# Expert weights fetched in 4 MB pieces from the fifth expert on, with four early-loaded pieces moved to other experts

## The reference

```python
def expert_block(args):
    tok, wr, e = args
    hb = xpad[tok] @ mlp1_w[e] + mlp1_b[e]              # 1024 -> 2048
    yb = clamped_swiglu(hb) @ mlp2_w[e] + mlp2_b[e]     # 1024 -> 1024
    return yb * wr[:, None].astype(yb.dtype)
```

## Time and profile before

| what | value |
|---|---|
| median of 3 runs | 1349.01 us (1348.27 to 1352.93) |
| the profiled execution's own time | 1347.37 us |
| its span, first to last instruction | 1345.6 us, so 1.8 us lie around it |
| mean granted TensorE clock | 0.981 of full speed |
| TensorE matmul busy | 1249.0 us (93%) |
| DVE, ACT, POOL busy | 357.0, 191.1, 60.3 us |
| read from HBM | 440.74 MB |

### The profile page before, as it was taken

How to read it: one execution, slowest core, us unless ns; L and a number is a source line. 1 busy time by engine, 2 the same in 40 slices (tenths; PEclk the granted TensorE clock), 3 DMA queues, 4 the chain that set the end, 5 groups by cost and what they waited for, 6 DMA issues and landing times.

```text
span 1345.6 us, 18997 instructions
## 1 busy us (share of the span) xinstructions
PE 1249.0 (93%) x7700; PEld 636.5 (47%) x7700; DVE 357.0 (27%) x843; ACT 191.1 (14%) x434; POOL 60.3 (4%) x107
## 2 busy tenths in 40 slices
PE   6999789879888999998989999999998999989897
PEld 5888677758776343332333334333233332323332
DVE  3555642332224522121212112212121111212111
ACT  2232234411221000000000000000000000000000
POOL 8200001101000000000000000000000000000000
PEclk9999889989998999999999999999999999999999
DMA  6333110009534999999999999999999999999996
GB/s 241 129 126 125 64 64 33 33 33 379 235 140 169 396 427 428 429 429 429 429 429 427 427 427 427 427 429 428 429 428 429 429 429 429 429 429 429 429 428 285
DMA packets 34916, 442.56 MB, mean 329 GB/s; under 512 B 3888, under 2 KB 4016, under 8 KB 5296
## 3 DMA queue, kind: packets, MB, share of 16 engines
q1 hardware_dynamic: 34704, 441.28, 78.4%
q0 software_dynamic: 160, 0.52, 0.1%
HBM read 440.74 MB, written 1.05 MB: 328 GB/s over the span
## 4 chain that ended last, share of the span: by engine, by line
PE 58%; DMA 34%; DVE 4%; issue 1%; ACT 1%; POOL 0%; SPq 0%; DVEq 0%; ACTq 0%
DMA sb_ring<-in_mlp_w 34%; PE ps L917 20%; PE ps L334 8%; PE ps L976 7%; PE ps L885 2%; PE ps L751 2%; PE ps L661 2%; PE ps L786 2%; PE ps L894 2%; PE ps L532 2%; PE ps L933 1%; PE ps L824 1%; PE ps L953 1%; PE ps L350 1%; PE ps L407 1%
## 5 line engine op out<-in xcount | busy, mean ns | idle before, releaser
L917 PE MATMUL ps<-sb_ring,sb_hT 128*64 128x512 f32 x1984 | 445.6, 597 | 35.4 <-DMA sb_ring<-in_mlp_w 34.4
L917 PEld LDWEIGHTS ps<-sb_ring,sb_hT 128*64 128x64 f32 x1984 | 134.7, 137 | 322.1 <-issue 252.8
L976 PE MATMUL ps<-sb_ring,sb_hT 128*64 128x512 f32 x1024 | 228.4, 596 | 0.0
L1491 DVE TENSOR_SCALAR sb_early<-ps 128x256 f32<-128x256 f32 x64 | 27.2, 425 | 645.1 <-PE ps L917 645.0
L976 PEld LDWEIGHTS ps<-sb_ring,sb_hT 128*64 128x64 f32 x1024 | 71.6, 137 | 133.3 <-issue 131.5
L1532 ACT ACTIVATE sb_early<-sb_early 128x256 f32<-128x256 f32 (+2 forms) x69 | 28.2, 408 | 524.1 <-DVE sb_early L1491 516.7
L334 PE MATMUL ps<-sb_hnT,sb_wsl 128*128 128x256 f32 x288 | 64.8, 386 | 3.7 <-DVE sb_hnT L1061 3.7
L1532 ACT ACTIVATE sb_early<-ps 128x512 f32<-128x512 f32 (+4 forms) x46 | 23.6, 515 | 287.9 <-PE ps L976 267.8
L885 PE MATMUL ps<-sb_early,sb_hnT 128*128 128x128 f32 x512 | 61.9, 281 | 0.8 <-DVE sb_early L1370 0.8
L334 PEld LDWEIGHTS ps<-sb_hnT,sb_wsl 128*128 128x128 f32 x288 | 55.8, 194 | 12.4 <-DVE sb_hnT L1061 4.1
L894 PE MATMUL ps<-sb_early 64*128 64x512 f32 x248 | 61.6, 615 | 0.0
(11 more groups left out here) (353 smaller groups left out, 1043.8 us busy)
## 6 DMA issues: line engine op xcount, KB each, us to landing
sb_ring<-in_mlp_w SPq DMA_DIRECT2D x186, 2048.0 KB, 22.0
sb_wsl<-in_w_front SPq DMA_DIRECT2D x31, 1024.0 KB, 4.8
sb_ring<-in_mlp_w SPq DMA_DIRECT2D x4, 1024.0 KB, 14.9
sb_wsl<-in_mlp_w SPq DMA_DIRECT2D x3, 1024.0 KB, 4.8
sb_wsl<-in_w_values SPq DMA_DIRECT2D x1, 1120.0 KB, 5.1
sb_hT<-in_x_T SPq DMA_DIRECT2D x2, 512.0 KB, 5.9
sb_wsl<-in_w_front SPq DMA_DIRECT2D x2, 512.0 KB, 6.8
sb_ox<-in_mem_T SPq DMA_DIRECT2D x1, 1024.0 KB, 11.5
```

What stands on the lines that cost most here:

```text
L917: mm = pe.matmul(psum[64 * half:64 * half + 64, 4 + n, :], xgT[:, k, SLOTS * par:SLOTS * par + SLOTS], w[:, at + 512 * half:at + 512 * hal ...
L976: mm = pe.matmul(psum[64 * o2:64 * o2 + 64, 7, :], actT[:, 2 * n + m, 64 * q:64 * q + 64], ring[:, at + 512 * o2:at + 512 * o2 + 512], sta ...
L1491: dve.tensor_scalar(gl, psum[:, 4 + n, 0:256], 7.0, None, ALU.min).then_inc(sem("glu"), 1)
```

## The change

From item 4 (`SINGLE`) on, SP joins pieces 0 and 1, 2 and 3, and 4 and 5 into one DMA of 4 MB each (128 rows of 32 KB). It issues such a DMA when both of its pieces are free, and TensorE waits for it only at the even piece. Items 0 to 3 keep 2 MB pieces. The pieces loaded ahead are now those of experts 8, 12, 16 and 20; in these items piece 1 comes alone. In the last item pieces 0 and 1 come as one DMA, the others as before. TensorE's program now has items 0 to 3 and 8 to 21 written out. In the last item `scatter` and the first transposes stand between pieces 2 and 3, and the second half's transposes between the two halves of the second layer.

```diff
-        AHEAD_AT = 10
+        AHEAD_AT = (8, 12, 16, 20)
+        SINGLE = 4
+        MIDDLE = AHEAD_AT[-1] + 2
...
+                ahead = sum(i >= at for at in AHEAD_AT) if stage == "middle" else 0
+                if c % 2 == 0:
+                    loads = i + 1 if c or stage == 0 else i + 2 - ahead
+                    pe.wait_ge(sem(f"piece_in_{c}"), loads * 16)
+                elif stage in (0, 1):
+                    pe.wait_ge(sem(f"piece_in_{c}"), (i + 1) * 16)
+                elif stage == "middle" and i in AHEAD_AT and c == 1:
+                    pe.wait_ge(sem("piece_in_1"), (SINGLE + ahead) * 16)
+                elif stage == "last" and c > 1:
+                    pe.wait_ge(sem(f"piece_in_{c}"), (SINGLE + 1) * 16)
...
                     if 1024 * (k + 1) % PIECE == 0:
                         mm.then_inc(sem("piece_used"), 1)
+                        if stage == "last" and n and k == 3:
+                            scatter(1 - par)
+                            turn_act(i, 0)
...
+                if stage == "last":
+                    pe.wait_ge(sem("selgT"), i + 1)
+                    second(i, 0, stage)
+                    turn_act(i, 1)
+                    second(i, 1, stage)
+                    return
...
-            item(0, 0, 0)
-            item(0, 1, 1)
+            for i in range(SINGLE):
+                item(i // 2, i % 2, min(i, 1))
...
-            with pe.Fori(1, AHEAD_AT // 2) as j:
+            with pe.Fori(SINGLE // 2, AHEAD_AT[0] // 2) as j:
                 for par in range(2):
-                    item(j, par, 1)
-            for a in range(4):
-                item((AHEAD_AT + a) // 2, a % 2, 1, ahead=a)
-                for bank in range(4) if a == 3 else ():
+                    item(j, par, "pairs")
+            for i in range(AHEAD_AT[0], MIDDLE):
+                item(i // 2, i % 2, "middle", ahead=AHEAD_AT.index(i) if i in AHEAD_AT else None)
+                for bank in range(4) if i == AHEAD_AT[-1] else ():
...
-            def item(i, e, which=range(PIECES)):
+            def pairs(i, e, which=(0, 2, 4)):
+
+                for c in which:
+                    sp.wait_ge(sem("piece_used"), i * PIECES + (c + 2 - PIECES))
+                    piece(e, c, at=(PIECE * c, PIECE * (c + 2)))
+
+            def singles(i, e, which=range(PIECES)):
+
                 for c in which:
                     sp.wait_ge(sem("piece_used"), i * PIECES + (c + 1 - PIECES))
                     piece(e, c)
...
+            for i in range(2, SINGLE):
+                singles(i, i)
+            with sp.Fori(SINGLE, AHEAD_AT[0]) as i:
+                pairs(i, i)
+            for i in range(AHEAD_AT[0], MIDDLE):
+                if i in AHEAD_AT:
+                    singles(i, i, (1,))
+                pairs(i, i, (2, 4) if i in AHEAD_AT else (0, 2, 4))
...
-            for c in range(PIECES - 1):
+            sp.wait_ge(sem("piece_used"), before_last * PIECES + 2)
+            piece(e, 0, at=(0, 2 * PIECE))
+            for c in range(2, PIECES - 1):
                 sp.wait_ge(sem("piece_used"), before_last * PIECES + (c + 1))
                 piece(e, c)
```

More of the change, by code:

```diff
@@ L921, in hidden, with turn_act, second, item @@
                         mm.then_inc(sem("piece_used"), 1)
+                        if stage == "last" and n and k == 3:
+                            scatter(1 - par)
+                            turn_act(i, 0)
                     elif stage == 0 and n == 0 and k == 1:
                         mm.then_inc(sem("half_used"), 1)
-            def item(j, par, stage, ahead=None, last=False):
+            def turn_act(i, n):
+                pe.wait_ge(sem("swiglu"), i * 2 + 2 + n)
+                pe.wait_ge(sem("act_out"), i * 2 + 1 + n)
+                for m in (2 * n, 2 * n + 1):
+                    mm = pe.transpose(psum[:, 6, m * P:(m + 1) * P], actv[:, m * P:(m + 1) * P], ident[:, :])
+                mm.then_inc(sem("act_turned"), 1)
+            def second(i, n, stage):
+                pe.wait_ge(sem("act_out"), i * 2 + 2 + n)
+                for q in range(2):
+                    for m in range(2):
+                        at = 16384 + 4096 * n + 2048 * q + 1024 * m
+                        if at % PIECE == 0:
+                            landed(i, at // PIECE, stage)
+                        if stage == "last" and n and q and m == 0:
+                            pe.wait_ge(sem("late_in"), 16)
+                        for o2 in range(2):
+                            mm = pe.matmul(psum[64 * o2:64 * o2 + 64, 7, :],
+                                           actT[:, 2 * n + m, 64 * q:64 * q + 64],
+                                           ring[:, at + 512 * o2:at + 512 * o2 + 512],
+                                           start=at == 16384, stop=at == 24576 - 1024)
+                        if (at + 1024) % PIECE == 0:
+                            mm.then_inc(sem("piece_used"), 1)
+            def item(j, par, stage, ahead=None):
                 i = j * 2 + par
@@ L948, in item @@
                     pe.wait_ge(sem("gate_taken"), 1)
[L949 to L962, removed]
+                if stage == "last":
[4 more added lines that the diff above has]
+                    return
+                turn_act(i, 0)
+                if first:
+                    for g in range(4):
+                        r = slice(NE * g, NE * g + NE)
+                        pe.matmul(psum[:, g, :], gateT[r, g // 2, :], bias2[r, :], start=True, stop=False,
+                                  skip_group_check=True)
+                else:
+                    scatter(1 - par)
+                turn_act(i, 1)
+                if par:
                     pe.wait_ge(sem("selected"), j + 2)
@@ L1993, in piece_ahead @@
                 lo = 2048 * half
-                sp.dma_start(aheads[n][half], a["mlp_w"][AHEAD_AT + n, :, lo:lo + 2048]) \
+                sp.dma_start(aheads[n][half], a["mlp_w"][AHEAD_AT[n], :, lo:lo + 2048]) \
                   .then_inc(sem(f"ahead_in_{n}"), 16)
@@ L2017, in _ @@
             piece(1, 0, at=(PIECE // 2, PIECE))
-            item(1, 1, range(1, PIECES))
-            with sp.Fori(2, AHEAD_AT) as i:
-                item(i, i)
-            for i in range(AHEAD_AT, AHEAD_AT + 4):
-                item(i, i, range(1, PIECES))
-            sp.sem_inc(sem("piece_in_0"), 16 * 4)
-            piece(AHEAD_AT + 4, 0)
-            item(AHEAD_AT + 4, AHEAD_AT + 4, range(1, PIECES))
-            with sp.Fori(AHEAD_AT + 5, NE - 2) as i:
-                item(i, i)
+            singles(1, 1, range(1, PIECES))
+            for i in range(2, SINGLE):
[6 more added lines that the diff above has]
+                pairs(i, i, (2, 4) if i in AHEAD_AT else (0, 2, 4))
+            sp.wait_ge(sem("piece_used"), MIDDLE * PIECES + (2 - PIECES))
+            sp.sem_inc(sem("piece_in_0"), 16 * len(AHEAD_AT))
+            with sp.Fori(MIDDLE, NE - 2) as i:
+                pairs(i, i)
             sp.wait_ge(sem("tabled"), 1)
@@ L2031, in _ @@
                 e = sp.value_load(tabi[0:1, bass.ds(i + 1, 1)], min_val=0, max_val=NE - 1)
-                item(i, e)
+                pairs(i, e)
             e = sp.value_load(tabi[0:1, bass.ds(last_item + 1, 1)], min_val=0, max_val=NE - 1)
             before_last = sp.value_load(tabi[0:1, 61:62], min_val=NE - 2, max_val=ITEMS - 1)
-            for c in range(PIECES - 1):
+            sp.wait_ge(sem("piece_used"), before_last * PIECES + 2)
+            piece(e, 0, at=(0, 2 * PIECE))
+            for c in range(2, PIECES - 1):
                 sp.wait_ge(sem("piece_used"), before_last * PIECES + (c + 1))
```

10 lines of the change are left out of this document (4 added, 6 removed).

## The result

The changed kernel takes 1352.11 us in the median, before 1348.69 us (20 runs each, measured side by side); the ratio is 1.0022, 95% interval 1.0012 to 1.0032, so 1.6 to 4.3 us slower. That is inside the 0.5% that I called no change, and inside the range. The sum in the prediction had +0.3 us. The profiled execution has a span of 1349.1 us, 3.5 us over that of before.

What follows compares the result with a forecast made beforehand. The weights' DMA queue, always holding work, was taken to bound the kernel. Terms -2.6 + 1.3 + 1.6 = +0.3 us on the profiled 1347.37 gave 1347.7, as a median 1349.3 us; range 1344.0 to 1354.0.

Steps and rivals of the forecast that it cites:

- 4 MB pieces: Joined DMAs from item 4 on: 78 joins save 33 ns each, -2.6 us, bounds -0.6 to -4.4.
- D: Rival on the joined DMAs: rows are cut into 16 KB packets, only completions are saved; +2.9, 1351.9 us; chance 0.18.
- C: Rival, faster: long DMAs flow at a better rate than the packet count says; 1346.6 or 1342 us; chance 0.13.
- its smaller case: In C: the step from 16 to 32 KB gives 0.7% on 78 DMAs, -5.3 us, 1346.6 in all.
- Items written out: TensorE's program: 12 more instruction packets in the DMA queues at 0.11 us each, +1.3 us, bounds 0.5 and 2.6.
- Moved early pieces: Pieces loaded ahead at items 8, 12, 16, 20: same bytes, queue never dry, so worth nothing by itself.
- The queue with 4 MB pieces: Steady items: tightest issue, pieces 4+5 of items 8, 12, 16, 20, has 1.9 us to spare; 0 us.
- rival B: Slower: the queue runs dry in the four early-loaded items; 1351.3, or 1355.7 us and more; chance 0.09.
- its two cases: In rival B: each place lacks 0.5 us, +2.0; or 3.5 us of delay at each place, +6.4.
- the mark of a wrong prediction: Rate in the windows 432 GB/s or more, or below 425 around items 8, 12, 16 or 20.
- The last item: Joined first pieces and new order: second layer ends 14.9 us after piece 3 is seen, before 13.3; +1.6 us.
- the second layer needs piece 4: Last item: piece 4 is there, 3.51 us more; second transposes and ACT's copy 1.0; last 3.51 end 14.9 after piece 3.

Runs made afterwards that it cites:

- waits half filled: U with the second half's bias matmuls started again twice in odd items' waits, except behind an early-loaded item; ratio to the kernel before 0.9991.
- U: Changed kernel with the whole last item as before (old order, pieces 0 and 1 as two DMAs); ratio to the kernel before 0.9998.
- odd items: U with the early-loaded pieces at items 9, 13, 17 and 21 in place of 8, 12, 16 and 20; ratio to the kernel before 0.9979.
- four kernels with the same middle: Changed kernel (1.0022), it with the last item's old order (1.0003), it with last pieces 0 and 1 as two DMAs (1.0022), and U (0.9998).

## Why the prediction was right, and where it was not

The call (no change within 0.5%) and the range held. The sum had +0.3 us, and +3.4 us were measured. That it came so near is partly luck: the gain of the change was put 3.3 us too small, and three losses were put too small as well (by 0.7 to 1.5, 1.7 and about 4 us), and these errors mostly cancel.

- **4 MB pieces.** Predicted -2.6 us, 33 ns for each of 78 DMAs. The loop's rates, 77.69 against 77.09 MB, make 9.71 of 9.79 us: 76 ns for each, -5.9 us, and splitting the DMAs cost 4.9 us. The packet count over 7 and 16 us was too coarse a ruler (its own bounds, -0.6 to -4.4, don't hold the measured value), and it carried the step from 8 to 16 KB over to 32 KB. Of the rivals, D (16 KB packets) is refuted by the packet count, though its time, 1351.9, is nearest to the measured one; of C its smaller case, 0.7% on these DMAs, happened. An item's period in the loop is 29.13 us, where I had said 29.27.
- **Items written out.** Predicted +1.3, measured 2.0 to 2.8 us at 1.0020 and 1.0021. The mechanism fits (the delay stands where the written-out items are and nowhere else), the size was short; the bound was 2.6. The Trainium skill, "Runtime: NRT & Kernel Launch", section "Instruction fetch mechanics", calls a block's price mostly hidden. TensorE shows no stall in 700 to 880 before, in agreement with it; for the time of this kernel, whose DMA queue is full, the 0.17 us or more of each packet is not hidden.
- **Moved early pieces.** Predicted 0 by themselves; with 2 MB pieces the two ratios agree (1.0020 and 1.0021), within some 2 us.
- **The queue with 4 MB pieces.** Predicted never dry, 1.9 us to spare. This step failed: rival B's place was right, and its price, about 4 us over the four places, lies between its two cases (2.0 and 6.4 us). The rate of 386 GB/s lies below the 425 that I had named as the mark of a wrong prediction, and the 432 of the loop (1110 to 1290) meets the mark on the other side. What took the spare time in part is TensorE's clock, which fell after two waits of 1.5 and 2.3 us; I had worked out such waits and not asked what they do to the clock. It is not all: groups without a fall still take 0.5 us more than the written-out items explain, with the waits half filled (clock 1.00 in the mean of that stretch) U still lacked 1.8 MB, and with odd items little was lost although the clock fell at the start of each group. By the groups of the profiles it is the larger part (1.9 us with a fall, 0.5 without); the kernel with the half filling, 0.9 us better than U with an uncertainty of 2, doesn't settle it. The margin was taken from one isolated 1 MB DMA and from mean landings. That the 16 queues end at different times, the first of them dry while the mean is not, is my guess, and not tested.
- **The last item.** Predicted +1.6 us, measured 3.3 in the profile. By the ratios, taking back the order alone gains 2.6 us, and taking back all of it 3.2 us. The step from "the second layer needs piece 4" forgot ACT: its copy stands behind the second half's activation in an order that the change left alone. The second layer ended 16.7 us after the landing of piece 3, where I had 14.9; 1.39 us are this wait, and 0.4 us lie in matmul groups and hand-overs that take a little longer than I had put them. I had also said that TensorE would wait about 5 us longer for the last item's first piece; it waited 0.43 us, because it was still at work on the item before until just ahead of the landing.

Sum after the fact: -5.9 (joined), +2.0 (written out), +3.3 (last item) and, for the profiles' +3.5 us, a remainder of +4.1 us for the dry queue. The changed kernel's own groups say the same: together they are 7.2 us over the loop's pace, and 0.8 us for each of the four is the share of the written-out items, which leaves 4.0.

## What to carry to other kernels

When one DMA queue sets the time, look for three things that no busy share shows: bytes that the program itself fetches, how much backlog is left where the consumer is latest, and which engine's order a moved instruction still depends on. Here the time of each group of items, landing to landing, showed the lost backlog better than the least issue-to-landing time, which was 12.1 to 14.2 us in four kernels with the same middle. Larger pieces gave a better rate and, issued and waited for as wholes, a smaller backlog; place what disturbs the backlog where the consumer is early. An instruction moved ahead gains nothing while its reader on another engine stays where it was.

## What the runs showed that I had not expected

- A DMA of 4 MB in rows of 32 KB moved 0.78% more in a second than two of 2 MB (77.69 and 77.09 MB in 180 us).
- TensorE's clock fell to its lower level for 3.4 us after waits of 1.52 and 2.26 us with 7 us of work between them, but not at each such pair: in the changed kernel two of five pairs from 560 to 1000 us passed at full clock. In the kernel before, with waits of up to 1.25 us, it never fell from 434 to 1290 us.
- In the kernel with odd early pieces the first group of four items lost nothing (642.72 to 754.44, 111.7 us), yet the stretch as a whole still lacks 1.4 MB. Its clock fell at the start of this group too (8.78 us); I did not find out what the rest is.
